# Exact three-part split of the normed tokens, on ScalarE and VectorE instead of GpSimd

## The reference

```
xn      = x * rsqrt(mean(x*x) + eps)              # 256 x 1024, f32
h       = xn * (1 + scale) * g + shift            # "modulate"
score   = sigmoid(h @ w_router)                   # 256 x 64
chosen  = the 8 best of score + bias, from the 4 best groups of 8
y       = shared_expert(h) + sum over the chosen experts of weight * expert(h)
x       = x + gate * y
```

## Time and profile before

| | |
|---|---|
| median of 3 runs | 2341.7 us (2339.08 to 2344.78) |
| span of the profiled execution | 2342.1 us (no other time of it is given) |
| TensorE matmuls | 2212.6 us, 94% of the span |
| VectorE | 853.2 us, 36% |
| ScalarE | 413.7 us, 18% |
| GpSimd | 59.1 us, 3% |

### The profile page before, as it was taken

The page is one execution under the profiler, slowest core; times in us unless marked ns, Lnnn a source line. Parts: engine busy times, 40 slices in busy tenths (PEclk is TensorE's granted clock), DMA queues, the critical chain, the costliest instruction groups (busy, mean ns, idle before and its releaser), DMA issues. The chain is left out here.

```text
span 2342.1 us, 41436 instructions
## 1 busy us (share of the span) xinstructions
PE 2212.6 (94%) x16176; PEld 1267.3 (54%) x16177; DVE 853.2 (36%) x2053; ACT 413.7 (18%) x882; POOL 59.1 (3%) x142
## 2 busy tenths in 40 slices
PE   4999999899999999979999989999999999699998
PEld 2844444555555555537454445555555555357465
DVE  2673323333333333236734243323323233244252
ACT  2223111111111111122231111111111111113122
POOL 1000002000000000000000020000000000101000
PEclk9999998999999999999999999999999999899999
DMA  8652742798898899786526427989989987623611
GB/s 289 210 203 80 279 155 114 291 364 352 356 360 357 347 362 365 287 309 194 183 100 259 171 106 300 364 347 358 366 345 358 364 347 285 185 88 98 215 65 54
DMA packets 165290, 599.18 MB, mean 256 GB/s; under 512 B 13052, under 2 KB 17760, under 8 KB 130656
## 3 DMA queue, kind: packets, MB, share of 16 engines
q1 hardware_dynamic: 163808, 595.10, 67.0%
q0 software_dynamic: 1408, 3.10, 0.6%
HBM read 597.11 MB, written 1.05 MB: 255 GB/s over the span
## 5 line engine op out<-in xcount | busy, mean ns | idle before, releaser
L1090 PE MATMUL banks<-weight_ring,qa_t 128*64 128x256 f32 x4224 | 481.7, 381 | 6.0 <-DVE qa_t L1783 3.3
L1090 PEld LDWEIGHTS banks<-weight_ring,qa_t 128*64 128x64 f32 x4224 | 298.4, 137 | 224.1 <-issue 88.6
L755 PE MATMUL banks<-weight_ring,h_t 128*128 128x512 f32 x768 | 340.4, 600 | 5.1 <-DMA weight_ring<-in_w_in 3.2
L1122 PE MATMUL banks<-conv_t,conv 128*128 128x512 f32 x528 | 254.8, 605 | 4.6 <-issue 3.4
L755 PEld LDWEIGHTS banks<-weight_ring,h_t 128*128 128x128 f32 x768 | 146.9, 192 | 191.0 <-issue 185.8
L1789 DVE TENSOR_TENSOR z<-banks,z 128x128 f32<-128x128 f32 x132 | 38.5, 291 | 559.4 <-ACT z L1351 559.4
L1078 PEld LDWEIGHTS banks<-z,sp_ 128*128 128x128 bf16 x6336 | 197.3, 98 | 30.7 <-issue 25.4
L1078 PE MATMUL banks<-z,sp_ 128*128 128x64 bf16 x6336 | 207.0, 193 | 2.9 <-DVEq L1774 2.9
L1781 DVE TENSOR_TENSOR qa_t<-banks,mod_col 128x512 f32<-128x512 f32 x132 | 91.3, 692 | 198.9 <-PE banks L1078 198.9
L2022 PE MATMUL banks<-weight_ring,h_t 128*128 128x512 f32 (+2 forms) x384 | 135.9, 514 | 11.3 <-DMA weight_ring<-in_w_in 9.6
L1122 PEld LDWEIGHTS banks<-conv_t,conv 128*128 128x128 f32 x528 | 89.9, 190 | 95.0 <-issue 93.0
(11 more groups left out here) (461 smaller groups left out, 1907.4 us busy)
## 6 DMA issues: line engine op xcount, KB each, us to landing
weight_ring<-in_w SPq DMA_DIRECT2D x264, 1024.0 KB, 9.2
weight_ring<-in_w_in SPq DMA_DIRECT2D x36, 2048.0 KB, 12.8
slots<-in_w SPq DMA_DIRECT2D x68, 1024.0 KB, 7.3
weight_ring<-in_w_mod SPq DMA_DIRECT2D x24, 2048.0 KB, 9.7
qk<-in_w SPq DMA_DIRECT2D x32, 1024.0 KB, 5.0
z<-in_w SPq DMA_DIRECT2D x32, 1024.0 KB, 10.9
weight_ring<-in_w_out SPq DMA_DIRECT2D x8, 2048.0 KB, 7.9
weight_ring<-in_w_in SPq DMA_DIRECT2D x10, 1024.0 KB, 7.7
```

The costliest lines, as they stand in the source:

```text
L755: mm = nc.tensor.matmul(bank[:, 0:cols], stationary[:, k, t * P:(t + 1) * P], w[:, k, 0:cols], start=(k == 0), stop=(k == KT - 1))
L1090: mm = nc.tensor.matmul(h_bank[g * SLOTS:(g + 1) * SLOTS, 0:FF], x_blk[:, j % 2, k, :], w13(j)[:, :, k, g * (FF // 2):(g + 1) * (FF // 2)] ...
L1122: mm = nc.tensor.matmul(y_bank[t][h][:], turned[:, i % PAIRS, t, P:2 * P], o_blk[:, h * CHUNK:(h + 1) * CHUNK], start=False, stop=True, sk ...
```

## The change

GpSimd's loop over the layers is removed, and with it both its casts and its subtractions. ScalarE casts part 0 of both tiles behind `modulate(1, l)` and ahead of the score, and then casts part 1 of each tile when VectorE has made its rest. VectorE makes the rests behind its own `modulate(1, l)`; the last remainder is written straight into part 2 as bf16. Two signals, `part_cast` and `rest_ready`, order the two engines. The semaphores of the constants at the start are merged to one for each engine that raises them, with the same waits. The computed values are the same.

```
-        table_ready, parts_ready = signal("table_ready"), signal("xn_parts_ready")
+        table_ready = signal("table_ready")
+        part_cast, rest_ready, parts_ready = signal("xn_part_cast", 2 * T), signal("xn_rest_ready", T), signal("xn_parts_ready")
+        xn_by_k = K.xn[:].rearrange("p t (q k) -> p t k q", k=KT)
...
             const_pool(pool)
-            with pool.Fori(0, DEPTH) as l:
-
-                pool.wait_ge(xn_ready[1].sem, xn_ready[1].at(l, T))
-                pool.sem_inc(wait_carrier, 1)
-                by_k = K.xn[:].rearrange("p t (q k) -> p t k q", k=KT)
-                for c in range(PARTS):
-                    for t in range(T):
-                        nc.gpsimd.tensor_copy(xn_parts[:, t, c], by_k[:, t] if c == 0 else xn_rest[:, t])
-                    pool.drain()
-                    if c < PARTS - 1:
-                        for t in range(T):
-                            nc.gpsimd.tensor_tensor(xn_rest[:, t], by_k[:, t] if c == 0 else xn_rest[:, t], xn_parts[:, t, c],
-                                                    ALU.subtract)
-                        pool.drain()
-                pool.drain().then_inc(parts_ready.sem, 1)
...
                 row_norm(1, l)
                 modulate(1, l)
+                for t in range(T):
+                    nc.scalar.activation(xn_parts[:, t, 0], xn_by_k[:, t], ACT.Copy).then_inc(part_cast.sem, 1)
+                for t in range(T):
+
+                    act.wait_ge(rest_ready.sem, rest_ready.at(l, t + 1))
+                    nc.scalar.activation(xn_parts[:, t, 1], xn_rest[:, t], ACT.Copy).then_inc(part_cast.sem, 1)
                 bank = full_of("rt", l)
...
                 norm_x(1, l)
                 modulate(1, l)
+                for t in range(T):
+
+                    dve.wait_ge(part_cast.sem, part_cast.at(l, t + 1))
+                    v.tensor_tensor(xn_rest[:, t], xn_by_k[:, t], xn_parts[:, t, 0], ALU.subtract).then_inc(rest_ready.sem, 1)
+                for t in range(T):
+
+                    dve.wait_ge(part_cast.sem, part_cast.at(l, T + t + 1))
+                    last = v.tensor_tensor(xn_parts[:, t, 2], xn_rest[:, t], xn_parts[:, t, 1], ALU.subtract)
+                last.then_inc(parts_ready.sem, 1)
                 dve.wait_ge(score_ready.sem, score_ready.at(l))
```

More of the change, by code:

```diff
@@ L179, in constants @@
     ramp_i, part_i = sb(SLOTS + 1, dt=I32), sb(1, dt=I32)
[L180 to L183, removed]
+    loaded, c_loaded, x_loaded = [sem(n) for n in ("loaded", "c_loaded", "x_loaded")]
+    from_pool, from_dve, from_act = [sem(n) for n in ("constants_from_pool", "constants_from_dve", "constants_from_act")]
+    counts_zeroed, inv_ready, masks_ready = 1, 2, 3
+    c_act_ready, ang_ready = 1, 2
+    c_sig_ready, tables_ready = 1, 2
     def sync_part(sp):
@@ L191, in sync_part @@
             sp.dma_start(K.x[:, t, :], A["x"][0, t * P:(t + 1) * P, :]).then_inc(x_loaded, 16)
-        sp.wait_ge(counts_zeroed, 1)
+        sp.wait_ge(from_pool, counts_zeroed)
     def pool_part(pool):
         nc.gpsimd.memset(K.pairs_before[:], 0)
-        pool.drain().then_inc(counts_zeroed, 1)
+        pool.drain().then_inc(from_pool, 1)
         for (first, count, _), theta, dim in zip(ROPES, (10000.0, 500000.0, 500000.0), (64, 32, 16)):
@@ L202, in pool_part @@
                 last = nc.gpsimd.memset(inv[:, first + i:first + i + 1], value)
-        last.then_inc(inv_ready, 1)
+        last.then_inc(from_pool, 1)
         nc.gpsimd.memset(K.eps[:], EPS)
@@ L248, in pool_part @@
                                 pattern=[[1, N_GROUPS], [-1, N_GROUPS]], channel_multiplier=0)
-        pool.drain().then_inc(masks_ready, 1)
+        pool.drain().then_inc(from_pool, 1)
     def vector_part(dve):
-        dve.wait_ge(c_sig_ready, 1)
+        dve.wait_ge(from_act, c_sig_ready)
         nc.vector.tensor_tensor(K.c_act[:], c_col[:], c_sig[:], ALU.mult)
-        dve.drain().then_inc(c_act_ready, 1)
+        dve.drain().then_inc(from_dve, 1)
         dve.wait_ge(loaded, 32)
@@ L259, in vector_part @@
         dve.drain()
-        dve.wait_ge(inv_ready, 1)
+        dve.wait_ge(from_pool, inv_ready)
         for first, count, which in ROPES:
@@ L286, in vector_part @@
         nc.vector.tensor_scalar(ang[:], ang[:], pi_in, -pi_in, ALU.min, ALU.max)
-        dve.drain().then_inc(ang_ready, 1)
-        dve.wait_ge(masks_ready, 1)
-        dve.wait_ge(tables_ready, 1)
+        dve.drain().then_inc(from_dve, 1)
+        dve.wait_ge(from_pool, masks_ready)
+        dve.wait_ge(from_act, tables_ready)
     def scalar_part(act):
         act.wait_ge(c_loaded, 16)
-        nc.scalar.activation(c_sig[:], c_col[:], ACT.Sigmoid).then_inc(c_sig_ready, 1)
-        act.wait_ge(ang_ready, 1)
+        nc.scalar.activation(c_sig[:], c_col[:], ACT.Sigmoid).then_inc(from_act, 1)
+        act.wait_ge(from_dve, ang_ready)
         nc.scalar.activation(K.sin[:], red[:], ACT.Sin)
         nc.scalar.activation(K.cos[:], ang[:], ACT.Sin)
-        act.drain().then_inc(tables_ready, 1)
+        act.drain().then_inc(from_act, 1)
         act.wait_ge(x_loaded, 16 * T)
-        act.wait_ge(masks_ready, 1)
+        act.wait_ge(from_pool, masks_ready)
     def tensor_part(pe):
-        pe.wait_ge(masks_ready, 1)
-        pe.wait_ge(c_act_ready, 1)
+        pe.wait_ge(from_pool, masks_ready)
+        pe.wait_ge(from_dve, c_act_ready)
     return sync_part, pool_part, vector_part, scalar_part, tensor_part
```

## The result

The changed kernel is slower by 0.28%: median 2349.39 us of 20 runs against 2344.48 us of 20 runs of the kernel before, made beside it; the ratio is 1.0028 with a 95% interval of 1.0014 to 1.0041, that is 6.6 us (3.3 to 9.6). One execution of each, 4383.46 and 2428.99 us, was a slow one and is left out of the ratio. The two medians alone differ by 4.9 us (1.0021), inside that interval. The prediction had 2346.9 us in a range of 2341 to 2352.5, slower by 5.2 us.

The account below looks back on a forecast made before the run. TensorE, with matmuls in flight 94% of 2342.1 us, bounds the kernel, so only its waits matter. A score 2.6 us later in each of two layers adds 5.2 us to 2341.7, giving 2346.9; range 2341 to 2352.5.

Parts of the forecast that it names:

- The place: Between second norm and shared expert, once per layer: TensorE's `shared_h` waits for ScalarE's score, held 0.56 us before the change.
- The terms of the chain: From `modulate` to the score: casts, remainders, then table load; score at 394.63 instead of 392.03, 2.6 us a layer.
- The stepped cast: ScalarE's first casts, reading `xn` in steps of 8 floats: 2.0 us each, against 1.05 packed.
- The stepped remainder: VectorE's first subtractions, reading `xn` in steps of 8 floats: 2.0 us each, against 1.22 packed.
- The high end for VectorE: Stepped subtraction at GpSimd's price, 2.6 us; with ScalarE's casts at 2.05, 3.8 us a layer, 7.6 in all.
- with only VectorE paying for the step: Case in the chain ahead of the score where only VectorE's stepped reads cost more: 1.75 us a layer.
- What was to cost nothing: VectorE's last two remainders, done before the score is ready; merged constants' semaphores; removal of GpSimd's 18.1 us a layer: no cost or gain.
- VectorE's relief: VectorE gets back 5.4 us a layer on L1659, L1660 and L1663 without GpSimd beside it; buys nothing.
- It fits under the router's product: Rival: casts and remainders fit ScalarE's 5.8 us of room; 0 to +3.5 us; chance 0.22.
- The clock makes it dearer: Rival: longer gap ahead of `shared_h` delays TensorE's clock rise; total 8.4 us, at worst 15.4; chance 0.15.
- the clock gives some back: Rival: clock rise stays at 398.0 while `shared_h` starts later; 1.3 us a layer back, total 2.6; chance 0.10.
- VectorE's relief reaches the path: Rival: VectorE's 5.4 us counts if TensorE waits for `chosen`; -5.6 us if all counts; next to no chance.

Follow-up runs that it names:

- the first experiment: The changed kernel with only the wait for bank `rt` moved from ahead of `shared_h` to ahead of the counting matmuls; ratio 0.9997 to the kernel before.
- the late wait: Wait for bank `rt` moved behind `shared_h`: on the kernel before, ratio 0.9998; on the changed kernel, 0.9997 in each of two sets.

## Why the prediction was right

**The place.** The prediction put the score on the path that sets the end. In the profiles that held to the letter: the one wait moved away took the whole loss of the stretch with it, and with the score made ahead of the split the loss was gone too.

**The terms of the chain.** Predicted 2.6 us a layer, measured 2.82 and 2.84. The stepped cast: taken 2.0, measured 2.08 median. The stepped remainder: taken 2.0, measured 2.07. These were prices without a row of their own, taken for VectorE from a stepped reduction of its own and for ScalarE from GpSimd's cast:

```profile
L1313 ACT ACTIVATE sp_<-xn x4: 2066/2082/2122, 387.4 to 1385.9; 128x1024 bf16<-128x1024 f32 x4
...
L1643 DVE TENSOR_TENSOR qk<-xn,sp_ x4: 2045/2074/2084, 389.5 to 1388.0; 128x1024 f32<-128x1024 f32 x4
...
L1647 DVE TENSOR_TENSOR sp_<-qk,sp_ x4: 1226/1228/1244, 393.4 to 1391.2; 128x1024 bf16<-128x1024 f32 x4
```

The three stepped instructions on the path were each some 0.05 to 0.08 us dearer, and the first began 0.12 us behind `modulate` where I had 0.06: that is the 0.2 us. The Trainium skill, "SBUF — State Buffer", in its note on cachelines, has a penalty for each access that crosses to a new 16-byte line. For a step of 8 floats the trace agrees on both engines, with a factor that the page doesn't give: 2.08 against 1.06 on ScalarE, 2.07 against 1.23 on VectorE. No run here reads in another step. The high end for VectorE, 2.6 from GpSimd, was too far. One sum of the bounds is off: with only VectorE paying for the step, the prediction's own terms give 1.65 us a layer and not 1.75. The kernel with packed casts had the score 1.8 us later than the kernel before.

**What was to cost nothing.** VectorE's last remainders ended at 395.90, 0.05 us before the score began, as forecast; the table load lay bare, 1.28 us; the merged semaphores and GpSimd's removal showed nothing. VectorE's relief was 6.15 us and not 5.4, because `biased` (0.29, had been 0.48) and the sum of the two group maxima behind it (0.19, had been 0.70) gained too; it bought nothing, as forecast.

**The rivals.** *It fits under the router's product* is what the chain does with both reads packed, and only then: gap 0.72 and 0.56. *The clock makes it dearer* and *the clock gives some back* find no support as effects of the longer gap: with gaps of 0.56, 3.04 and 7.27 us the half clock reached 5.4, 5.6 and 5.3 us into `shared_h` in layer 0. It does vary from one profile to the next (3.2 to 6.1 us into `shared_h` over all the kernels with a gap), with no visible order by the length of the gap; one profile of each kernel can't show more. Without any gap it ended earlier, 2.7 us into `shared_h` in layer 0 of the first experiment (row below), and 2.0 to 4.2 over the three profiles with the late wait. *VectorE's relief reaches the path*: no, 10.5 us of room in the changed kernel.

```profile
386.90:393.50 6.60, 6.60 (x23) 5.12 (x23) 6.05 (x4) 5.49 (x5) 0.00 (x0) 0.50 0.00 0
```

What the sum did not have is the 0.9 us by which the stretch around the chain was longer in the profiled execution and about 1 us elsewhere, within what the clock does from run to run. A chance near one half for "slower" was fair: the 5.7 us of loss in the chain is 0.24%, and the two sets of runs of the changed kernel gave 0.28% and 0.15%. That the total came out within 1.5 us of the forecast is in part luck, since the interval of the first set alone is 6 us wide. What the prediction got right beyond luck is the chain, to 0.2 us a layer.

## What to carry to other kernels

Work that an idle engine does slowly under cover is free; before it is moved to engines that seem idle, look whose result is queued behind the new place, and add up the chain between the engines against the cover (here 8.4 us against 5.8 in the forecast), not each engine's busy share. Price the step before the move: with steps of 8 floats the casts took twice the packed time (2.08 against 1.06 us on ScalarE, 2.04 against 1.04 on GpSimd), VectorE's subtraction 1.7 times and GpSimd's 1.2 times (2.61 against 2.15). And when an engine waits for a buffer, ask which instruction writes it first: the wait for `rt` stood one product too early. With it behind `shared_h` the stretch took 82.3 to 82.4 us, whether GpSimd made the split or ScalarE and VectorE did ahead of the score.

## What the runs showed of the hardware

I had not expected to find a large part of the spread of the totals in the second stack, which the change doesn't touch. In four of the profiled executions (both reads packed, remainders packed, the kernel before with the late wait, and the second run of the changed kernel with it) TensorE runs at half clock for 10 to 17 us in a place where the others run at full. Windows of the second run of the changed kernel with the late wait, and of the kernel before at the same instructions (columns as above):

```profile
2147.30:2164.20 16.90, 15.10 (x52) 11.45 (x52) 2.20 (x5) 1.79 (x3) 0.00 (x0) 0.50 0.00 0
```

```profile
2144.00:2162.00 18.00, 15.40 (x80) 10.51 (x81) 4.71 (x13) 2.19 (x5) 0.00 (x0) 1.00 0.00 1
```

In this profile of the changed kernel with the late wait the clock fell at 2147.2. TensorE had run sixteen products of 64 columns since 2145.41 (L2155 here, L2152 of the kernel before), behind 1.12 us of idle. In layer 0 of the kernel before it fell at 387.7, 1.5 us into the router's products of 64 columns, behind 1.84 us of idle.

From the first of these products in the second stack to the next layer's transposes the kernel before takes 39.24 us (2144.70 to 2183.94) and these four 43.5, 46.4, 46.4 and 46.4: 4.3 to 7.2 us more, as much as the whole change costs. The same kernel does it in one profile and not in another: of the two profiles of the changed kernel with the late wait the first takes 39.24 us here and the second 46.4, and their spans are 2338.1 and 2351.2 us. So no edit decides it alone.

An edit may still change how often it happens. The 101 times of the kernel before fall in two groups with a hole between: up to 2346.7 us, and 28 of them from 2348.9. The profiled executions with 46.4 us whose kernels were run twelve times were of the upper group of their set. In the changed kernel's two sets only 2 of 31 times stand above such a hole (2361.31 and 2362.96, all others up to 2351.7). In the three sets with the late wait 18 of 36 do, from 2346.7 up. Within the lower groups the changed kernel run again has a median of 2347.50 and its form with the late wait one of 2341.97, 5.5 us less, near the expected 6 that the medians of all runs don't show. The groups were cut after the times were seen, and what makes their shares differ was not tested; what decides whether the clock falls there was not found.
